# Interleaving the two weight tiles of a block, and moving the moving operands to another place modulo 256 bytes

## The reference, cut to what matters

```python
x = first_block(x, mem, ...)      # h @ w_in, o @ w_out, xa_wq .. xa_wo, mlp_w1, mlp_w2
x = second_block(x, c_2, ctx_2, ...)   # h @ w_in, latent projections, w_out, w_up, w_down
```

## Time and profile before

| | |
|---|---|
| median of the runs | 3080.9 us |
| the profiled execution, its own time | 3077.71 us |
| its span, first to last instruction | 3075.9 us |
| mean granted TensorE clock | 0.970 |
| PE busy | 2901.8 us, 94% |
| PEld busy | 2838.5 us, 92% |
| DVE busy | 2096.0 us, 68% |
| ACT busy | 1331.7 us, 43% |
| matmuls of the line 448 | 21744 |

### The profile page before, as it was taken

The page is one execution under the profiler, slowest core; times in us unless marked ns, Lnnn a source line. Parts: engine busy times, 40 slices in busy tenths (PEclk is TensorE's granted clock), DMA queues, the critical chain, the costliest instruction groups (busy, mean ns, idle before and its releaser), DMA issues.

```text
span 3075.9 us, 55206 instructions
## 1 busy us (share of the span) xinstructions
PE 2901.8 (94%) x23858; PEld 2838.5 (92%) x23858; DVE 2096.0 (68%) x2934; ACT 1331.7 (43%) x1646; POOL 5.1 (0%) x13
## 2 busy tenths in 40 slices
PE   7998888999999899999999989988998999999998
PEld 7998787999998899999999979967598999999998
DVE  6988654698977877676766775454457665665665
ACT  4445323443433453444435444434345543554453
POOL 0000000000000000000000000000000000000000
PEclk9999898999999999999999989998999999999999
DMA  5554102577664677777777745522144565555553
GB/s 203 188 169 165 55 1 80 204 254 260 245 227 168 240 289 275 280 274 268 287 268 267 282 140 178 190 98 96 55 156 153 195 199 196 191 195 196 192 195 117
DMA packets 160451, 591.58 MB, mean 192 GB/s; under 512 B 17840, under 2 KB 17840, under 8 KB 159696
## 3 DMA queue, kind: packets, MB, share of 16 engines
q1 hardware_dynamic: 159264, 579.93, 53.4%
q0 software_dynamic: 944, 8.12, 0.7%
HBM read 585.88 MB, written 2.10 MB: 191 GB/s over the span
## 4 chain that ended last, share of the span: by engine, by line
PE 86%; DVE 10%; ACT 2%; issue 1%; DMA 1%; SPq 0%; DVEq 0%; ACTq 0%
PE bank L448 76%; DVE wlo L1218 2%; PE bank L712 1%; DVE ev L1237 1%; DVE modacc L1423 1%; PE bank L469 1%; PE bank L463 1%; PE bank L616 1%; PE bank L473 1%; DVE tmp L1373 1%; PE bank L614 1%; PE bank L608 1%; DVE ev L1340 1%; PE bank L687 1%; ACT whi L823 1%
## 5 line engine op out<-in xcount | busy, mean ns | idle before, releaser
L448 PE MATMUL bank<-act,whi 128*128 128x256 f32 x10144 | 1784.4, 281 | 59.7 <-DVE wlo L1218 20.2
L448 PEld LDWEIGHTS bank<-act,whi 128*128 128x128 f32 x10144 | 1560.0, 191 | 65.4 <-issue 34.1
L1218 DVE TENSOR_TENSOR wlo<-raw,whi 128x1024 fp32r<-128x1024 f32 x906 | 1098.1, 1223 | 530.2 <-ACT whi L823 528.4
L448 PE MATMUL bank<-act,wlo 128*128 128x256 f32 x5072 | 1421.7, 280 | 0.0
L823 ACT ACTIVATE whi<-raw 128x1024 fp32r<-128x1024 f32 x906 | 948.2, 1057 | 898.0 <-PE bank L448 897.4
L448 PEld LDWEIGHTS bank<-act,wlo 128*128 128x128 f32 x5072 | 969.4, 191 | 0.0
L448 PE MATMUL bank<-hid,whi 128*128 128x256 f32 x3456 | 602.5, 279 | 0.0
L448 PEld LDWEIGHTS bank<-hid,whi 128*128 128x128 f32 x3456 | 524.5, 188 | 0.0
L448 PE MATMUL bank<-hid,wlo 128*128 128x256 f32 x1728 | 482.1, 279 | 0.0
L1204 DVE SCALAR_TENSOR_TENSOR modacc<-modraw,small,modacc 128x512 f32<-128x512 f32 x480 | 348.6, 747 | 11.0 <-DMA modraw<-mods 5.6
L448 PEld LDWEIGHTS bank<-hid,wlo 128*128 128x128 f32 x1728 | 328.8, 190 | 0.0
(11 more groups left out here) (269 smaller groups left out, 1545.3 us busy)
## 6 DMA issues: line engine op xcount, KB each, us to landing
raw<-stream SPq DMA_DIRECT2D x906, 512.0 KB, 4.4
modraw<-mods SPq DMA_DIRECT2D x192, 512.0 KB, 4.1
h<-x_t SPq DMA_DIRECT2D x4, 512.0 KB, 6.3
memV<-mem_t POOLq DMA_DIRECT2D x1, 2048.0 KB, 8.6
tmp<-ctx_t POOLq DMA_DIRECT2D x1, 2048.0 KB, 12.5
out_t<-tmp SPq DMA_DIRECT2D x4, 512.0 KB, 2.6
cz<-catt POOLq DMA_DIRECT2D x1, 1216.0 KB, 12.2
bias<-na_bias POOLq DMA_DIRECT2D x1, 1024.0 KB, 5.1
```

The source lines that it names most:

```text
L448: mm = pe.matmul(b[:, hf * T:(hf + 1) * T], lhs, rhs, start=(kc == 0 and hf == 0 and n == 0), stop=(kc == ph.chunks - 1 and n == 2), skip_ ...
L1218: ve.tensor_tensor(wlo[:, at % SPL_N, :], raw[:, at % RAW_N, :], whi[:, at % SPL_N, :].bitcast(F32), ALU.subtract).then_inc(split_done, 1)
```

## The change

The host writes the two weight tiles of a block alternately: column 0 of the first, column 0 of the second, column 1 of the first, and so on. A weight load then reads every second float, 128 of them over 1024 bytes instead of 128 in a row over 512 bytes. Flipped phases keep the old order, and in the phases with `ncol=P` there is one tile, so step and order stay. `act_skew` goes from 112 floats to 32, which moves `act` and everything declared after it 320 bytes down.

```diff
-        sb("act_skew", [P, 112])
+        sb("act_skew", [P, 32])
         act = sb("act", [P, 2, DC, T], F32R)
...
-                                            lhs = wx[:, buf, ci * ph.ncol + hf * P:ci * ph.ncol + (hf + 1) * P]
+                                            cols = wx[:, buf, ci * ph.ncol:(ci + 1) * ph.ncol]
+                                            lhs = cols.rearrange("p (n a) -> p a n", a=ph.ncol // P)[:, hf, :]
                                             rhs = src[:, ax, c0 + kc, :]
...
     w = w.reshape(ph.slots_per_block, ph.per_slot, P, ph.nblocks, ph.ncol)
+    if not ph.flip:
+        w = w.reshape(w.shape[:-1] + (ph.ncol // P, P)).swapaxes(-1, -2).reshape(w.shape)
     return w.transpose(3, 0, 2, 1, 4).reshape(ph.slots, P, SLOT)
```

## The result

| | before | after |
|---|---|---|
| median, us | 3080.19 | 3182.17 |
| lowest to highest | 3073.06 to 3082.37 (4 runs) | 3173.0 to 3183.92 (4 runs) |
| profiled execution, span | 3075.9 | 3182.1 |

The ratio is 1.0329, 95% interval 1.0303 to 1.0355. The forecast was 3013, with 2995 to 3145 as its range.

The account below looks back on a forecast made before the run. Line 448's matmul spacing was taken to bound the kernel. Savings of 17 us (fast matmuls) and 56 us (slow), less 5 us off the path, made 68 us: 3013 us against the median, range 2995 to 3145.

Parts of the forecast that it names:

- What bounds the kernel: Whole kernel: time is line 448's 21,744 matmuls times their spacing, plus some 500 us the change doesn't touch.
- The floor and what lies above it: Line 448: undisturbed loads need 111.7 ns; its matmuls run 1.6 or 6.1 ns above that, 68 us in all.
- The price of a load with step two: Line 448's unflipped weight loads: bounded by 111.7 and 223 ns, lower end taken, so no added time.
- The prediction's own signs: Profile after, if step two costs time: weight loads longer than 192 ns, or counts under 342 at 1460 to 1500 us.
- That load and stream never meet at distance 128: Line 448, unflipped: both walk 1024 bytes evenly over about 112 ns, staying 128 apart; spacing falls to 111.7 ns.
- the two paces: Line 448's spacings before, 113.3 and about 118 ns; one pace was forecast everywhere outside the flipped phases.
- The skew: Moving act and hid from 192 to 128 modulo 256 from the weights; tiles behind keep their distances: 0 us.
- The spread costs: Each line 448 load: touching 1024 bytes instead of 512 doubles the loss; 3130 or 3154 us, 25%.
- Nothing happens: Line 448: paces come from PE's instruction order, not memory, so step and skew don't matter; 3081 us, 15%.
- All at the fast pace: Line 448: the layout only stops the slow meeting, 9,200 matmuls gain 4.5 ns, 41 us; 3040 us, 12%.
- under the floor: Line 448: if the load doesn't set 111.7 ns, the stream needs 106.7; 2913 us, half of it 2960; 5%.
- a load halves its speed: Line 448's loads with step two take 223 ns, 2,160 us more; 5,240 us, 5%.

Follow-up runs that it names:

- the other kernel at 192: Kernel before with act_skew at 48 floats instead of 112, the same distance of 192 modulo 256 bytes: 3080.94 us (1 run).

## Why the prediction was wrong

**What bounds the kernel: right.** The time moved with line 448's spacing and with nothing else.

**The floor and what lies above it: right in size.** The forecast took 68 us for everything above 111.7 ns. The kernel before took 3077 to 3082 us in most comparisons, and with the stream standing still 3005.39, some 72 to 77 less, and that kernel left the flipped matmuls as they were. The Trainium skill's rule of two read ports that don't take from one another ("TensorE: Matmul & The Clock Gate", the step "LDWEIGHTS") doesn't hold for these operands: 111.6 ns with the stream on one place, 113.3 to 120.1 with the stream walking, and in memv 113.6 or 120.2 by where the load starts, the stream unchanged.

**The price of a load with step two: this step failed.** The prediction bounded it by 111.7 and 223 ns and took the lower end, since "eight bytes a column is what the moving stream already gets through in the time of one loaded column". That the stream does it doesn't make the load do it. Beside a stream that stands still the load takes 117.7 ns. The two kernels with the standing stream differ by 111 us for this alone, 6.1 ns x 20,000 = 122 us less what lies off the path. The true price was near the lower end, 5% of the way to the upper, and that 5% is more than the whole gain looked for. The prediction's own signs for this step being wrong are both there: loads over 192 ns (194 and 198) and fewer than 342 matmuls in 40 us.

**That load and stream never meet at distance 128: failed as well.** With step two the walking stream adds 121.0 - 117.7 = 3.3 ns at 128, and 2.4 ns at 0 and at 192. That is less than the 8.4 ns that distance 0 costs loads in a row (120.1 - 111.7), but more than the fast pace paid before (1.6). So the two paces did go, as forecast, but for one above both (121.0, in a few stretches 120.2).

**The skew: costed at nothing for the other tiles, rightly, but wrongly as part of a cure.** TensorE's busy time outside the one line stayed within 2 us. For loads in a row 192 is the best distance tried; leaving it for 128 costs 2.3% by itself. The flipped phase memv went from 117.8 (38.28/325 at 752 to 790 us) to 118.5 ns; the prediction read 118 to 119 for before, from a window that starts ahead of the phase's first matmul.

**The rivals.** "The spread costs", 3130 to 3154 us, was on the right side and short by 28 us. Its place was right, each load, and the bytes that a load spans do count; but it put the cost on the meeting with the stream, and 6.1 ns of it are there beside a standing one. "Nothing happens" fell with the skew alone, which moved the time by 2.3% with every instruction in its old order. "All at the fast pace" and "under the floor" fell with the result: no window of the kernel after shows 113.3 ns, and none of any kernel that computes the whole result a spacing of line 448 below that. The rival that a load halves its speed with step two named what happens at step four.

**Sum after the fact.** Unflipped matmuls at full clock: load +6.1 ns each, stream +3.3 instead of +1.6 or +6.1. Fast ones: 10,800 x (6.1 + 3.3 - 1.6) = 84 us; slow ones: 9,200 x (6.1 + 3.3 - 6.1) = 30 us; together 114 of the 116 us that the line's busy time grew by. The 3.3 is the measured 121.0 less the 117.7, so this splits the loss and doesn't test it.

**Still open.** Why a stretch takes the fast or the slow pace at distance 192. In the kernel before one change comes with line 463, but no run changed that line. What sets a load's 111.7 ns in a row, and what the pair does to one another within a matmul, no run shows. Other distances than multiples of 32 weren't tried. No version that computes the whole result beat the kernel before.

## What to carry to other kernels

Before giving an operand a step, measure the load with that step beside a stream that stands on one float: it costs one kernel more and separates the load's own price from most of the contention. A layout that must save 2 to 6 ns of a matmul can't afford a load 6 ns longer. Where weights and activations are both read in a row, try the start modulo 256 bytes in steps of 32 or 64: here 192 was worth 1.0 to 2.7% against every other place, the 1.0 (distance 64) and the 2.7 (distance 0, against the other kernel at 192) from single runs.

## What the runs showed of the chip

- Beside a stream that stands on one float, a load of 128 fp32r columns takes 111.7 ns or some 58 ns for every 512 bytes that it spans in a partition, whichever is more: 117.7, 173.5 and 233.2 ns for steps two, three and four.
- With loads in a row and 256 moving columns the spacing depends on where the moving operand starts from the loaded one, modulo 256 bytes: from 113.3 to 120.1 ns. At 64 and at 192 two paces, 113.3 and 117.8, occur with the same addresses.
- At half clock the spacing is 213 ns with step one and step two alike, with 64 moving columns.
- Shortening the moving operand from 256 to 64 columns made the kernel slower, 5043 us for 3077: the granted clock fell to 0.60 on average, though PE was busy 97% of the span where it had been 94%. The same kernel with 256 columns of one float kept 0.97.
